# Placing the SBUF tiles of a hybrid decoder layer anew, with every TensorE operand at a multiple of 512 bytes

## The reference, cut to what matters

```python
hn = rms_norm(h, mix_pre_g)
q, k, v, u, gv = split(hn @ w_in)                  # 1024 x 2560, five pieces of 512
attn_out = moba_attention(rope(q), rope(k), v)     # 8 heads x 64, causal
gmlp_out = gmlp_spatial_gating(gelu(u), gelu(gv))  # 128 x 128 per group of 64 channels
h = h + rms_norm(concat(norm(attn_out), norm(gmlp_out)) @ w_o)
hn = rms_norm(h, mlp_pre_g)
h = h + rms_norm(square(relu(hn @ w_up)) @ w_down) # 1024 x 4096 and back
gate = sigmoid(h @ w_ple_gate + b_ple_gate)
h = h + rms_norm((p @ w_ple) * gate)               # p: 512 x 256
```

## The kernel before

| tiles | remainder by 512 | remainder by 128 |
|---|---|---|
| actT, mixT (with qT), w_hi, w_lo, t ring (in mixT's place), h, work, wsT, gv | 128 | 0 |
| a_hi3, a_lo3 (in junk's place) | 128 | 0 |
| a_hi0 to 2, a_lo0 to 2, pT_hi, pT_lo, kT_hi, kT_lo, v, probs, probsT, attn, u, acc (all in the area) | 192 | 64 |
| ident, ident_bf | 256 | 0 |
| at_rows, stat, rowsum | 64 | 64 |

## Time and profile before

### The profile page before, as it was taken

The page is one execution under the profiler, slowest core; times in us unless marked ns, Lnnn a source line. Parts: engine busy times, 40 slices in busy tenths (PEclk is TensorE's granted clock), DMA queues, the critical chain, the costliest instruction groups (busy, mean ns, idle before and its releaser), DMA issues.

```text
span 613.2 us, 7823 instructions
## 1 busy us (share of the span) xinstructions
PE 600.3 (98%) x2922; PEld 489.4 (80%) x2922; DVE 403.8 (66%) x603; ACT 313.2 (51%) x541; POOL 82.5 (13%) x152
## 2 busy tenths in 40 slices
PE   8999999999999999999999999999999999999995
PEld 6888888777767878888888888888888888888884
DVE  5476444567755793766867757757778578668654
ACT  6754544656454755554534625544546355534422
POOL 1176332000001120001001001010010010001011
PEclk9999999999999999999999999999999999999998
DMA  8654332223000359554737556638365566234011
GB/s 309 253 195 141 105 103 69 68 69 104 1 2 26 110 181 322 139 210 93 190 137 158 137 156 153 220 75 201 138 134 145 160 151 210 93 130 168 13 69 69
DMA packets 23653, 82.90 MB, mean 135 GB/s; under 512 B 2752, under 2 KB 3136, under 8 KB 23104
## 3 DMA queue, kind: packets, MB, share of 16 engines
q1 hardware_dynamic: 18000, 60.83, 28.2%
q0 software_dynamic: 4032, 14.68, 14.0%
q10 hardware_dynamic: 1584, 6.90, 2.9%
HBM read 78.20 MB, written 4.19 MB: 134 GB/s over the span
## 4 chain that ended last, share of the span: by engine, by line
PE 88%; DVE 5%; ACT 3%; issue 1%; DMA 1%; POOL 1%; SPq 0%; DVEq 0%; ACTq 0%; POOLq 0%
PE psum L1607 28%; PE psum L1612 28%; PE psum L1611 28%; PE psum L1661 2%; PE psum L1774 1%; PE psum L1754 1%; DVE stat L548 1%; DMA first_raw_a<-weights_dram 1%; DVE w_lo L440 1%; ACT work L1113 1%; PE psum L1675 1%; ACT probs L1064 1%; ACT w_hi L935 0%; DVE psum L615 0%; DVE psum L543 0%
## 5 line engine op out<-in xcount | busy, mean ns | idle before, releaser
L440 DVE SCALAR_TENSOR_TENSOR w_lo<-raw,cols,w_hi 128x512 fp32r<-128x512 f32 x112 | 86.3, 813 | 46.7 <-ACT w_hi L935 46.5
L1612 PE MATMUL psum<-actT_hi,w_lo 128*128 128x512 f32 x256 | 99.8, 390 | 0.0
L1611 PE MATMUL psum<-actT_lo,w_hi 128*128 128x512 f32 x256 | 99.8, 390 | 0.0
L1607 PE MATMUL psum<-actT_hi,w_hi 128*128 128x512 f32 x256 | 99.7, 389 | 0.0
L935 ACT ACTIVATE w_hi<-raw,cols 128x512 fp32r<-128x512 f32 x112 | 74.3, 713 | 42.8 <-PE psum L1607 25.4
L1607 PE MATMUL psum<-w_hi,actT_hi 128*128 128x512 f32 (+1 forms) x232 | 90.6, 390 | 1.3 <-DVE w_lo L440 1.2
L1612 PE MATMUL psum<-w_hi,actT_lo 128*128 128x512 f32 (+1 forms) x232 | 88.7, 383 | 0.0
L1611 PE MATMUL psum<-w_lo,actT_hi 128*128 128x512 f32 (+1 forms) x232 | 88.7, 382 | 0.0
L1607 PE MATMUL psum<-t_hi,a_hi 128*128 128x512 f32 x212 | 83.6, 394 | 0.0
L1611 PE MATMUL psum<-t_lo,a_hi 128*128 128x512 f32 x212 | 83.6, 394 | 0.0
L1612 PE MATMUL psum<-t_hi,a_lo 128*128 128x512 f32 x212 | 83.6, 394 | 0.0
(11 more groups left out here) (169 smaller groups left out, 917.8 us busy)
## 6 DMA issues: line engine op xcount, KB each, us to landing
raw<-weights_dram SPq DMA_DIRECT2D x66, 512.0 KB, 3.6
raw_o<-weights_dram SPq DMA_DIRECT2D x23, 512.0 KB, 4.0
raw_x<-weights_dram POOLq DMA_DIRECT2D x21, 512.0 KB, 5.4
raw_x<-weights_dram SPq DMA_DIRECT2D x9, 512.0 KB, 5.4
raw_o<-weights_dram POOLq DMA_DIRECT2D x7, 512.0 KB, 9.0
ple_spill<-ple ACTq DMA_DIRECT2D x1, 2048.0 KB, 9.4
out_dram<-h SPq DMA_DIRECT2D x7, 256.0 KB, 2.0
xT_raw<-xT_dram SPq DMA_DIRECT2D x4, 256.0 KB, 5.8
```

Source lines behind the costliest of these rows:

```text
L440: nc.vector.scalar_tensor_tensor(out=w_lo[:, place_at, :], in0=source, scalar=gain, in1=high, op0=ALU.mult, op1=ALU.subtract).then_inc(sla ...
L1607: begin = nc.tensor.matmul(out, a_hi, b_hi, start=first, stop=False, skip_group_check=read_between)
L1611: nc.tensor.matmul(out, a_hi, b_lo, start=False, stop=False, skip_group_check=read_between)
L1612: return nc.tensor.matmul(out, a_lo, b_hi, start=False, stop=last, skip_group_check=read_between)
```

## The change

The small tiles are placed first, and the top is then rounded up to a multiple of 2,048 bytes ahead of h. ident starts at 16,896 and h at 20,480, both multiples of 512; at_area becomes 188,416, a multiple of 512 as well. So a_hi, a_lo, pT, kT, v, probs, probsT, attn, u, actT, mixT, w, t, h, work, wsT, gv and ident all lie at remainder 0; ident_bf, which only the warm-up uses, lies at 128; the shared place of rope_tmp and at_rows is at 0. mean_of_w is at 128. at_rows now shares its bytes with rope_tmp, whose last use is long before. No instruction, wait, order or shape is changed; what moves are addresses, by 3,968 bytes for the large tiles and by -192 for those of the area.

```diff
--- before.py
+++ after.py
@@ -198,7 +198,23 @@
             return nc.alloc_sbuf_tensor_at(name, shape, dt, offset=at)
 
         base = nc.sbuf_base
-        top[0] = -(-base // 32) * 32
+
+
+        top[0] = -(-base // 128) * 128
+        ident_bf = place("ident_bf", [P, P], BF16)
+        rowsum = place("rowsum", [P, TT * PAIRS, 2])
+        assert top[0] % 512 == 0
+        ident = place("ident", [P, P])
+        at_rope_tmp = top[0]
+        rope_tmp = place("rope_tmp", [P, 2, HEADS, 2 * HALF_ROPE])
+        at_rows = place("at_rows", [P, P], at=at_rope_tmp)
+        causal = place("causal", [P, P])
+        rope_sb = place("rope_sb", [P, TT, 2, 2 * HALF_ROPE])
+        stat = place("stat", [P, 114 + len(GATE_TILES)])
+        cols = place("cols", [P, columns.shape[1]])
+        mean_of_w = place("mean_of_w", [P, 1])
+        rinv = place("rinv", [P, HEADS])
+        top[0] = -(-top[0] // (2 * KIB)) * 2 * KIB
         h = place("h", [P, TT, D])
         actT_hi = place("actT_hi", [P, KD, SEQ], F32R)
         actT_lo = place("actT_lo", [P, KD, SEQ], F32R)
@@ -216,17 +232,6 @@
         work = place("work", [P, 2, W])
         at_junk = top[0]
         junk = place("junk", [P, D])
-        cols = place("cols", [P, columns.shape[1]])
-        rope_sb = place("rope_sb", [P, TT, 2, 2 * HALF_ROPE])
-        rope_tmp = place("rope_tmp", [P, 2, HEADS, 2 * HALF_ROPE])
-        ident = place("ident", [P, P])
-        ident_bf = place("ident_bf", [P, P], BF16)
-        causal = place("causal", [P, P])
-        mean_of_w = place("mean_of_w", [P, 1])
-        rinv = place("rinv", [P, HEADS])
-        at_rows = place("at_rows", [P, P])
-        stat = place("stat", [P, 114 + len(GATE_TILES)])
-        rowsum = place("rowsum", [P, TT * PAIRS, 2])
         at_area = top[0]
         kT_hi = place("kT_hi", [P, PAIRS, SEQ], F32R)
         kT_lo = place("kT_lo", [P, PAIRS, SEQ], F32R)
```

## The result

The changed kernel takes 611.09 us (median of 4 runs, 610.52 to 612.09) against 614.80 (4 runs): ratio 0.9941, 95% interval 0.9924 to 0.9958. Measured again with more runs, 611.12 against 615.36: ratio 0.9926 (0.9913 to 0.9939). The profiled execution's own time went from 614.93 to 610.52, by 4.41 us, where 4.48 were forecast.

The account below looks back on a forecast made before the run. TensorE, busy for 98%, was taken as the bound through its start-to-start distance; gains of 3.65 + 0.45 + 0.15 + 0.08 + 0.15 = 4.48 us gave 610.3 us, 8 in 10 range 609.2 to 615.1.

Parts of the forecast that it names:

- Down products: MLP down products: slow ones and the slow matmuls following them reach 226.7 ns, stretch 289.25 to 285.60 us, gain 3.65.
- Plain down tiles: Plain down tiles: six tiles go from 16.77 to 16.32 us, gain 0.45; the last two gain 0.15.
- Large tiles at remainder 0: fp32r matmuls already at 226.7 ns, such as the gate's, keep that pace when moved to remainder 0: gain 0.
- Other engines and transfers: VectorE and ScalarE do not care about placement, 0; transfers 0, with 0.3 us either way.
- Ahead of the MLP: Work before the first down product: p @ w_ple gains 0.08 us and the scores 0.15.
- p @ w_ple: Its 48 matmuls speed up by 0.32 us, but a wait for hn absorbs the earlier gain; 0.08 counted.
- Scores: Attention scores, with moving kT in the area, run at the longer pace; some 15 ns a unit gained, 0.15 us counted.
- nothing moves: Rival: the area is slow for a reason other than its remainder, or both only coincide; 614.8 us, chance 0.10.
- Everything at remainder 128 now: Fast fp32r matmuls at remainder 128 keep 226.7 ns at remainder 0; gain 0, bounds -10.7 to +6.6 ns.
- Second step down: Rival: position within 256 or 512 bytes counts, so every fp32r matmul gains; 594.7 or 585.3 us, chance 0.12.
- Waits take it back: Rival: splits become late, likeliest ScalarE's t_hi behind a weight transfer; half the gain, 612.5 us, chance 0.04.
- Aligned starts collide: Rival: stationary and moving reads meet at 512-byte starts, slowing fast fp32r matmuls to 233.3 ns; 626.6 us, chance 0.06.

Follow-up runs that it names:

- experiment 2: Changed kernel with h and everything behind it 64 bytes higher, both operands at 64 by 128, distance 0; 610.52 us, ratio 0.9926 to the kernel before.
- experiment 3: Changed kernel with stationary a of ring places 0, 1, 2 put 32, 96 and 192 bytes higher; 614.40 us in one run.
- experiment 4: Changed kernel with stationary a of ring places 0, 1, 2 put 64, 128 and 256 bytes higher; 614.05 us in one run.
- experiment 8: Kernel before with only 192 bytes put ahead of the area, making the distance 256; 610.82 us, ratio 0.9928.
- experiment 9: Changed kernel with only the low parts a_lo of ring places 0 to 2 at distance 64 by 256; 613.89 us in one run.
- experiment 6: Changed kernel with mixT and the moving t ring 64 bytes higher, everything else at 0; 614.12 us in one run.
- experiment 1: Kernel before with only 64 bytes put ahead of the area; 614.75 us against 615.22, ratio 0.9993.
- experiment 7: Changed kernel itself, measured again with more runs; 611.12 us against 615.36 for the kernel before, profiled execution 613.17.
- experiment 5: Changed kernel with stationary a of ring places 0, 1, 2 put 160, 224 and 512 bytes higher; 615.88 us in one run.
- the ladder: Changed kernel with stationary a of ring places 0 to 2 at stepped byte offsets from the moving t; three kernels, 614.40, 614.05 and 615.88 us.

## Why the prediction was right, and which step of it was not

**The bound** was read rightly: PE stayed busy for 98%, its waits unchanged, and the gain stands where the starts moved closer.

**Down products**: 3.65 us forecast, 3.62 measured. **Plain down tiles**: 0.45 and 0.45 for the six; the last two take 2.81 and 2.73 us in place of 2.88 and 2.79, a gain of 0.13 for a forecast of 0.15. **Large tiles at remainder 0**: 0 taken, 0 measured (21.76 us for the gate's 96). **Other engines and transfers**: 0 taken; VectorE's busy time in the MLP is 203.65 in place of 204.05.

**Ahead of the MLP**, 0.23 us was forecast, and no gain is shown. The first down product does start at 246.68 in place of 246.82; but in experiments 2, 3, 4, 8 and 9, whose fp32r distances up to there are 0 by 256 as in the changed kernel, it starts anywhere from 246.03 to 247.11. *p @ w_ple*, from its first matmul to the first up tile, takes 13.93 us in place of 13.94 (13.88 in experiments 2 and 8): the gain ahead of the wait was given back in it, as forecast, and the last twelve matmuls with the step to the next tile gained 0.04 where 0.08 was forecast.

*Scores*: here a step of the prediction failed. It took 0.15 us from the earlier trace rows, reading 0.24 us from one pair's start to the next as the longer pace. From start to start, the 96 matmuls take 10.75 us at distance -64 before, 10.73 at 0 in the changed kernel, and 10.71 at +64 in experiment 6, where the stationary qT lies in the moved mixT. Unit 12, from its first pair to the transposes behind it, in these three kernels in this order:

```profile
165.51 0.66 PE L1754 MATMUL psum<-ident,probs 128*128 128x128 f32 x4
```

```profile
164.48 0.50 PE L1612 MATMUL psum<-kT_hi,mixT_hi 64*128 64x512 f32 x2
...
165.38 0.44 PE L1759 MATMUL psum<-ident,probs 128*128 128x128 f32 x2
```

```profile
164.52 0.50 PE L1614 MATMUL psum<-kT_hi,mixT_hi 64*128 64x512 f32 x2
...
165.42 0.44 PE L1761 MATMUL psum<-ident,probs 128*128 128x128 f32 x2
```

With the 164.61 of the earlier trace rows that is 0.90 us each time. So these matmuls, two side by side over 64 partitions each, do not follow the distance; why is open. The prediction's argument against "nothing moves", that the scores show the same 6.7 ns, fails with it; the one from pT stands.

**What was wrong** is the reason given for the step "Everything at remainder 128 now" and for the two distances: "0 by 128 is what the fast class has in common". Experiment 1 has 0 by 128 everywhere and no gain; experiment 2 has 64 by 128 everywhere and the whole gain. What the two classes of the earlier trace rows differ in is the distance from the moving operand's start to the stationary one's, by 256 bytes. The half sentence "both operands keep their distance to each other" named it, as a side remark. The forecast came out since the change makes both right at once: it takes the distance from 64 to 0. That was luck. With this reason alone, I would have put 64 bytes ahead of the area and gained nothing.

**The size.** 610.3 was forecast, 4.48 below the median of 614.79. The profiled execution kept the 4.48 within 0.1 us, partly by chance: 4.20 of its 4.41 stand in the MLP and the plain down tiles (4.25 forecast), and the rest is within what executions differ by ahead of the MLP. The median, 611.1, is 0.8 above the forecast. The runs of the changed kernel spread over 1.6 us where those of the kernel before spread over 0.6 in the same measurement.

The long execution of experiment 7 shows two sources of such a spread. Of its extra, 1.2 us lie in the MLP, at the two waits shown there. The other 1.4 lie ahead of it, and there the granted clock fell (the column PEclk, third from the right; first experiment 7, then the changed kernel as profiled first):

```profile
177.00:182.00 5.00, 5.00 (x28) 3.88 (x24) 2.80 (x6) 0.94 (x2) 0.55 (x1) 0.66 0.01 3
177.00:182.00 5.00, 5.00 (x37) 3.92 (x33) 3.40 (x8) 1.84 (x5) 0.55 (x1) 1.00 0.01 3
```

In these 5 us TensorE starts 28 matmuls in place of 37, with 0.66 of the upper level, 2.4 GHz, as it spends part of them at the lower one, 1.2 GHz. Between 172 and 177 us it was busy for 3.6 of 5 us in both, so its work just before does not tell the two apart. The profiled executions of experiments 1 and 5 have the same fall at the same place (0.71 and 0.68). So has, by all signs, the kernel before: each of its five executions above 616.0 us lists a mean granted clock of 0.995, as experiment 1's 617.12 does; their traces were not kept. Experiment 1 is the kernel before but for 64 bytes, so the fall of the clock is no work of the change. Whether the change makes the two waits more frequent is open.

**The rivals.** *Second step down*: refuted; neither remainder 0, nor 64, nor any distance of the ladder gave less than 226.7 ns. The 215.8 ns that the Trainium skill gives (TensorE: Matmul & The Clock Gate, Back-to-back issue gap) was reached at no placement tried; the measurement decides. *Nothing moves*: refuted. The 16-byte lines of the Trainium skill (SBUF — State Buffer, Door 1) do not tell the paces apart: all of the ladder's steps start on such a line and differ by up to 7.4 ns. *Waits take it back*: not seen in the first profiled execution, MLP stretch 285.63 at 100% busy; in that of experiment 7 it did happen in part, 1.2 of 3.6 us, by the path that the prediction named, t_hi behind a weight transfer. *Aligned starts collide*: refuted by the gate's 21.76 us, the same at remainder 0 as at 128 before and at 64 in experiment 2. (Its price counted the last two plain down tiles, 24 matmuls, among the fast ones: 1,752 in place of 1,776, which moves it by 0.2 us.)

## What to carry to other kernels

Where TensorE is busy all the time, compare the distance from start to start among stretches of the same shape before believing that it is at its best; two paces of one shape point to the operands' places. For fp32r matmuls of this form (512 moving columns, 128 stationary ones, all 128 partitions), keep the starts of stationary and moving tiles equal by 256 bytes, which a pad ahead of a group of tiles does; alignment of each to 64 or 128 is neither needed nor enough. And a change that moves several things at once can be right for another reason than the one given: the one-line experiments tell.

## What the runs showed of the hardware that was not expected

The start-to-start time of fp32r matmuls with 512 moving columns and 128 stationary ones depends on where the two tiles start relative to each other: 226.7 ns at distance 0 by 256, 229.0 at 192, 232.6 to 234.1 at 32, 64, 96, 128, 160 and 224. It has a sign: +64 gives 233.3 and -64 gives 228.9. The scores, over 64 partitions, do not show it (10.71 to 10.75 us for 96 at -64, 0 and +64). After a change of pace, some matmuls keep the longer one before the shorter is reached (the up tile of 5.47 us in the earlier trace rows against 5.43). Transposes of fp32 did not show it: in the kernel before they are 109 ns apart both for work and h (distance 128 by 256 from ident) and for attn, probs and u (192), and in the changed kernel, at distance 0, 109 ns as well. In three of the eleven profiled executions (experiments 1, 5 and 7) the granted clock fell for part of the stretch from 177 to 182 us, which made the attention some 1.6 us longer (103.3 us in place of 101.7, experiments 5 and 7). Why 226.7 is the least, when 512 columns at 2.4 GHz are 213.3 ns, stays open; that a weight load and the stream beside it meet in SBUF fits the pattern but was not shown.
